# Expert slots divided by token tile, and a spare buffer that holds one expert matrix of each layer

## The chip, the core and the metric

One core of one Trainium2 chip runs the whole program. The time is the device time of one execution in microseconds. The engines are TensorE (PE, its weight loads are shown as PEld), VectorE (DVE), ScalarE (ACT), GpSimd (POOL) and SyncE (SP), which here issues nearly all DMAs. All data is fp32.

## What is computed

The reference is an encoder of two layers over 256 tokens of width 1024. Each layer adds a mixer (layer 0: gated spatial mixing beside windowed attention; layer 1: dilated attention), a cross-attention to 256 memory tokens, and a mixture of experts. The last is what the change touches:

```python
def hier_moe(h, w_grp, b_grp, w_exp, b_exp, w_gate, w_up, w_down):
    t = h.reshape(-1, d)
    grp = jnp.argmax(g_logits, axis=-1)
    top_v, top_i = lax.top_k(e_sel, MOE_TOP_K)
    ...
    for gi in range(MOE_GROUPS):
        hid = jax.nn.silu(jnp.einsum('td,edf->tef', t, w_gate[gi])) * jnp.einsum('td,edf->tef', t, w_up[gi])
        hid = hid * gate[:, gi, :, None]
        y = y + jnp.einsum('tef,efd->td', hid, w_down[gi])
```

Each of the 16 experts of a layer has three matrices (gate and up 1024x512, down 512x1024) of 2.097 MB each, 48 matrices a layer. A token goes to two experts.

## The kernel before

Tokens lie in two tiles of 128 (`h`, `nrm`, dimension t). Weights come through a **ring** of six slots of 16 KB per partition, one matrix each. `load(n, ...)` on SP waits until slot n - 6 has been used (`ring_used`) and issues the DMA; TensorE waits in `arrived` for its landing, and its last product that reads the slot raises `ring_used`. SP's loads stand in one order for the whole program, so a load that waits holds back all behind it. The same slots serve both mixers, the cross-attentions and the experts.

**The expert stage** (`experts(l)` on each engine). The router gives every token two experts; `pos{l}` counts, by products with a triangular and an all-ones matrix (5 matmuls, in two tiles), which place a token has in its expert's list. VectorE's `selectors_of(g)` builds `sel`, for each tile the 0/1 matrix from 128 tokens to the 4 x 64 slots of a group's experts. `gather(g, j)` multiplies token rows by it: 4 matmuls of 256 columns into bank 6 or 7 (a "piece"), both tiles summed. VectorE or ScalarE copies a piece, scaled, into `xg`. Pieces use the two banks in turn, so a piece waits for the copy of the last but one.

Then come eight **duos** q of two experts, two duos to a group g. In a duo TensorE computes gate products into bank 0 and up products into bank 1 (`products`, 16 matmuls each, 64 slots of either expert in half of the bank's partitions), then two pieces of the next group's gathers, four flips (transposes) of `hid` into bank 2, and the down products into banks 3 and 4. ScalarE computes silu and copies the left half of the output (512 columns) to `ysb`, VectorE computes `hid` and copies the right half. Each duo's outputs are added to the tokens by four **scatters** (two tiles, two halves, 128x512 each, line 1362), with `scat`, the transposed and gated selectors of the duo. They run during the next duo, three behind its gate products (`before_up`; in duos 6 and 7 behind the up products, `before_turn`) and one behind its flips; VectorE adds each to `h` (line 1657). The outputs of duo 7 are scattered at the end of the stage (`halves_of_first` and three more), and the next norm waits for them.

Where an expert has more than 64 tokens, a flag (`ovf`) lets a second pass run over all experts with their weights loaded anew. It doesn't run here.

In the trace a matmul of 128x512 or 128x256 is two instructions, one of flips is one. Line 1009 is the helper `mm`, 1012 the helper `flip`, 752 ScalarE's copy.

## Time and profile before

| | |
|---|---|
| time of the runs, us | 1103.21, 1104.18, 1105.98 (median 1104.18) |
| profiled execution: its own time | 1105.44 |
| its span, granted TensorE clock | 1103.6, 0.984 |
| PE busy | 1040.9 (94%) |
| DVE, ACT busy | 269.2 (24%), 170.6 (15%) |
| read from HBM | 280.76 MB, 255 GB/s over the span |
| chain that ended last | PE 90%, DMA 5%, DVE 3% |
| expert stage of layer 0, products | from 243.85 to about 471.8 us |
| expert stage of layer 1, products | from 861.78 to about 1089.7 us |

The page gives one execution: the busy time of each engine, the span cut into 40 slices of 27.6 us, the DMA queues, and the chain of work that ended last. The trace behind it has every instruction with its start, what it waited for, and the clock that TensorE was granted.

### The profile page before, as it was taken

What the parts mean: (1) busy time and instruction counts of PE and PEld (TensorE: products, weight loads), DVE (VectorE), ACT (ScalarE), POOL (GpSimd) and SP (SyncE); (2) the same over time, 40 slices, a digit from 0 to 9 for tenths busy, and PEclk for the clock granted to TensorE, in tenths of its full rate; (3) what the DMA queues carried; (4) which work ended last, traced back from release to release, by engine and by line L of the source; (5) the groups of instructions that cost most, each with busy time, mean ns of one, the idle gap of its engine ahead of it and who ended that gap; (6) DMA issues with size and microseconds to landing.
All of it is one profiled execution on the core that took longest, in us unless ns stands there. A gap on an engine that the chain in (4) does not pass through costs nothing.

```text
span 1103.6 us, 10945 instructions
## 1 busy us (share of the span) xinstructions
PE 1040.9 (94%) x4480; PEld 619.9 (56%) x4480; DVE 269.2 (24%) x688; ACT 170.6 (15%) x354; POOL 11.1 (1%) x21
## 2 busy tenths in 40 slices
PE   4999998999999999899999999999978999999986
PEld 4567566464444443377788877886555544334432
DVE  2424332340111111132212221122335111111114
ACT  2014302031111110011101120101022210111101
POOL 1020000000000000000000000000000000000000
PEclk8999999999999999999999999999998999999998
DMA  9684234228999999998094490874322499999991
GB/s 332 225 292 153 77 153 171 77 77 361 425 428 428 426 427 429 373 249 210 1 254 117 88 280 2 207 265 171 120 110 77 194 429 422 426 429 429 427 426 55
DMA packets 108359, 282.54 MB, mean 256 GB/s; under 512 B 3847, under 2 KB 81751, under 8 KB 96025
## 3 DMA queue, kind: packets, MB, share of 16 engines
q1 hardware_dynamic: 106864, 278.17, 68.0%
q0 software_dynamic: 1168, 3.40, 1.0%
q8 instruction: 34, 0.56, 0.2%
q10 hardware_dynamic: 280, 0.31, 0.1%
q14 instruction: 13, 0.10, 0.0%
HBM read 280.76 MB, written 1.11 MB: 255 GB/s over the span
## 4 chain that ended last, share of the span: by engine, by line
PE 90%; DMA 5%; DVE 3%; issue 1%; ACT 0%; DVEq 0%; SPq 0%
PE banks L1009 83%; PE banks L1362 5%; DMA ring<-expert_w_up_in 3%; PE banks L1012 3%; DMA ring<-xkv_w_in 1%; DVE nrm L1779 0%; DVE mx L1771 0%; DVE h L1649 0%; DVE nrm L1722 0%; DVE nT L665 0%; DVE scratch L1813 0%; ACT nT L663 0%; DVE xv L692 0%; DVE scratch L2020 0%; DVE xkT L699 0%
## 5 line engine op out<-in xcount | busy, mean ns | idle before, releaser
L1009 PE MATMUL banks<-ring,scratch 128*64 128x512 f32 (+1 forms) x1792 | 454.1, 599 | 13.7 <-issue 6.0
L1009 PEld LDWEIGHTS banks<-ring,scratch 128*64 128x64 f32 (+1 forms) x1792 | 169.3, 146 | 283.2 <-issue 281.1
L1009 PE MATMUL banks<-nT,ring 128*128 128x256 f32 x1040 | 227.0, 379 | 1.5 <-DVE nT L665 0.6
L1009 PEld LDWEIGHTS banks<-nT,ring 128*128 128x128 f32 x1040 | 196.6, 190 | 28.7 <-issue 1.9
L1009 PE MATMUL banks<-ring,nT 128*128 128x384 f32 (+2 forms) x320 | 102.7, 476 | 0.0
L752 ACT ACTIVATE scratch<-banks 128x512 f32<-128x512 f32 (+1 forms) x76 | 42.6, 583 | 282.4 <-PE banks L1012 167.8
L1009 PEld LDWEIGHTS banks<-ring,nT 128*128 128x128 f32 x320 | 57.4, 190 | 37.7 <-issue 7.7
L1657 DVE TENSOR_TENSOR h<-banks,h 128x512 f32<-128x512 f32 x56 | 38.7, 691 | 117.3 <-PE banks L1362 117.3
L1009 PE MATMUL banks<-scratch,nrm 128*128 128x256 f32 x256 | 61.1, 394 | 2.4 <-DVE scratch L1948 1.2
L1009 PEld LDWEIGHTS banks<-scratch,nrm 128*128 128x128 f32 x256 | 48.8, 195 | 19.0 <-issue 12.5
L1362 PE MATMUL banks<-scratch 128*128 128x512 f32 x112 | 56.8, 619 | 0.0
L2013 DVE TENSOR_TENSOR scratch<-banks,scratch 128x512 f32<-128x512 f32 x16 | 16.8, 1052 | 152.3 <-PE banks L1009 152.3
L1009 PE MATMUL banks<-scratch 128*128 128x128 f32 (+4 forms) x324 | 49.0, 324 | 4.1 <-issue 2.3
L1009 PEld LDWEIGHTS banks<-scratch 128*128 128x128 f32 (+2 forms) x324 | 40.3, 185 | 17.5 <-issue 8.2
L851 ACT ACTIVATE scratch<-banks,gains 128x256 f32<-128x256 f32 x56 | 23.5, 470 | 158.2 <-PE banks L1009 158.2
L2020 DVE TENSOR_SCALAR scratch<-banks 128x512 f32<-128x512 f32 x16 | 11.1, 692 | 116.1 <-PE banks L1009 116.1
L1009 PE MATMUL banks<-scratch,ring 128*128 128x256 f32 x128 | 31.0, 404 | 5.4 <-DMA ring<-xkv_w_in 5.4
L1012 PE MATMUL banks<-cst,scratch 128*128 128x128 f32 x180 | 26.7, 286 | 8.5 <-DMA scratch<-mem_in 8.5
L1362 PEld LDWEIGHTS banks<-scratch 128*128 128x128 f32 x112 | 17.9, 189 | 28.6 <-issue 18.1
L1012 PEld LDWEIGHTS banks<-cst,scratch 128*128 128x128 f32 x180 | 23.0, 149 | 16.7 <-issue 14.0
L1009 PEld LDWEIGHTS banks<-scratch,ring 128*128 128x128 f32 x128 | 25.9, 204 | 10.3 <-DMA ring<-xkv_w_in 5.8
L1649 DVE TENSOR_TENSOR h<-banks,h 128x512 f32<-128x512 f32 x24 | 16.6, 691 | 53.2 <-PE banks L1009 53.1
(148 smaller groups left out, 421.9 us busy)
## 6 DMA issues: line engine op xcount, KB each, us to landing
ring<-expert_w_gate_in SPq DMA_DIRECT2D x32, 2048.0 KB, 13.1
ring<-expert_w_up_in SPq DMA_DIRECT2D x32, 2048.0 KB, 14.3
ring<-expert_w_down_in SPq DMA_DIRECT2D x32, 2048.0 KB, 11.7
ring<-odd_w_in_in SPq DMA_DIRECT2D x72, 512.0 KB, 7.1
ring<-xkv_w_in SPq DMA_DIRECT2D x4, 2048.0 KB, 11.8
ring<-even_w_in_in SPq DMA_DIRECT2D x3, 2048.0 KB, 20.3
ring<-even_w_out_in SPq DMA_DIRECT2D x2, 2048.0 KB, 16.2
ring<-xq_w_in SPq DMA_DIRECT2D x2, 2048.0 KB, 11.8
```

The lines of the kernel that those rows point to most:

```text
L752: return nc.scalar.activation(dst, src, ACT.Copy)
L851: last = nc.scalar.activation(xg[:, g % 2, c, :], pbank(k)[:, i * 256:(i + 1) * 256], ACT.Copy, scale=gtok[:, l, c:c + 1])
L1009: return giving_back(nc.tensor.matmul(dst, lhsT, rhs, start=start, stop=stop))
L1012: return giving_back(nc.tensor.transpose(dst, src, ident))
L1362: nc.tensor.matmul(pbank(k)[:, :], rows, ysb[:, q % 2, f * 512:(f + 1) * 512], start=True, stop=True).then_inc(piece_ready, 1)
L1649: v.tensor_tensor(r, b[:, :], r, ALU.add).then_inc(resid, 1)
L1657: v.tensor_tensor(r, pbank(k)[:, :], r, ALU.add).then_inc(evac[k % 2], 1)
L2013: v.tensor_tensor(hid.rearrange("p c f -> p f c"), bank[1].rearrange("p (f c) -> p f c", c=FC), silu.rearrange("p (f c) -> p f c", c=FC), ...
L2020: v.tensor_scalar(ysb[:, q % 2, 512:D], bank[4][:, :], 1.0, None, ALU.mult).then_inc(y_dve, 1)
```

## The change

1. **Slots by tile.** The 64 slots of an expert are divided, 32 (`SHARE`) for either token tile. A gather of a tile then fills only its own columns: 4 matmuls of 128 columns in a piece, nothing summed. `sel` has half the size. The flag is raised where an expert has more than 32 tokens in one tile.
2. **Scatter once per group.** As only 32 x 4 = 128 slots of a group belong to a tile, the outputs of both duos of a group lie in one tile of 128 rows in `ysb[:, t]`, and four scatters serve a group. They run in duos 2, 4 and 6 (`closes_group`) and at the end. `scat` has two transposed blocks per group in place of four.
3. **Output copies by tile.** ScalarE copies tile 0's rows, VectorE tile 1's: for either expert of the duo 32 partitions by 1024 columns from banks 3 and 4.
4. **Positions.** Two matmuls of 32 columns in place of five of 16.
5. **Spare slot.** The room that this frees, the last 16 KB of `scratch`, holds matrix 6 of each layer (gate of the third expert, used in duo 1). Its load stands ahead of the stage's ring loads in SP's order, waits in layer 0 for the mixer's last outputs and gated rows, in layer 1 for the use of the spare matrix of layer 0. The ring carries 47 matrices of a layer, in the old order.
6. The second pass takes one tile at a time.

```diff
 SLOTS = 64
+SHARE = SLOTS // TILES
...
+        assert a.at <= SCRATCH - SLOT
+        spare_slot = scratch[:, SCRATCH - SLOT:SCRATCH]
...
+        MATRICES = 3 * EXPERTS
+        SPARE = 6
+        W_ODD = W_MOE0 + MATRICES - 1
...
+        def closes_group(q):
+            return q >= 2 and q % 2 == 0
+
         def before_up(q):
-            return range(3) if 1 <= q < 6 else ()
+            return range(3) if closes_group(q) and q < DUOS - 2 else ()
 
         def before_turn(q):
-            return range(3) if q >= 6 else ()
+            return range(3) if closes_group(q) and q == DUOS - 2 else ()
...
+                if l == 0:
+                    sp.wait_ge(ya_set, 2)
+                    sp.wait_ge(e_pv_ps, PAIRS)
+                else:
+                    sp.wait_ge(gate_ps, 2)
+                sp.dma_start(spare_slot, rows_of(SPARE)).then_inc(spare_in, 16)
+                for m in range(MATRICES):
+                    if m != SPARE:
+                        load(ring_index(l, m), matrix(l, m), rows_of(m))
...
+        def expert_rows(half, i, t):
+
+            to, at = SHARE * (2 * half + i), SLOTS * i + SHARE * t
+            return ysb[to:to + SHARE, t, :], banks[at:at + SHARE, 3:5, :].rearrange("p b n -> p (b n)")
...
-                    copy(ysb[:, q % 2, 0:512], bank[3][:, :]).then_inc(y_act, 1)
+                    for i in range(2):
+                        dst, src = expert_rows(half, i, 0)
+                        last = copy(dst, src)
+                    last.then_inc(y_act, 1)
...
                     for i in range(2):
                         for t in range(TILES):
-                            last = mm(pbank(k)[:, i * 256:(i + 1) * 256], nrm[:, t, 2 * j + i, :],
-                                      sel[:, t, 256 * g:256 * (g + 1)], t == 0, t == 1)
+                            at = i * SEQ + t * P
+                            last = mm(pbank(k)[:, at:at + P], nrm[:, t, 2 * j + i, :], sel[:, t, P * g:P * (g + 1)], True, True)
...
                 selectors_of(0)
-                v.tensor_reduce(most, pbank(k)[:, 32:48], AX.X, ALU.max).then_inc(evac[PIECES[k] % 2], 1)
+                v.tensor_reduce(most, pbank(k)[:, 32:64], AX.X, ALU.max).then_inc(evac[PIECES[k] % 2], 1)
                 selectors_of(1)
                 piece_out(dve, k)
-                step(v.tensor_scalar(most, most, SLOTS + 0.5, None, ALU.is_gt))
+                step(v.tensor_scalar(most, most, SHARE + 0.5, None, ALU.is_gt))
```

How the instructions of layer 0's expert stage stand on TensorE, first before. Rows 1 and 2 of each piece are the positions and the first group's gathers; after them `ring,scratch` are gate, up or down products (16 each), `scratch,nrm` gathers, `cst,scratch` flips, and line 1362 (1402 in the change) scatters. The piece of before goes to the end of duo 2's gathers:

```order
L1009 MATMUL banks<-scratch,cst 128x16 x5
L1009 MATMUL banks<-scratch,nrm 128x256 x16
L1009 MATMUL banks<-ring,scratch 64x512 x32
L1009 MATMUL banks<-scratch,nrm 128x256 x8
L1012 MATMUL banks<-cst,scratch 128x128 x8
L1009 MATMUL banks<-ring,scratch 64x512 x32
L1362 MATMUL banks<-scratch 128x512 x3
L1009 MATMUL banks<-ring,scratch 64x512 x16
```

Behind it stand, in every duo, three scatters, gathers, flips and the fourth scatter. In the change the same place, up to duo 1, and then, behind a break, duos 2 and 3:

```order
L1056 MATMUL banks<-scratch,cst 128x32 x2
L1056 MATMUL banks<-scratch,nrm 128x128 x16
L1056 MATMUL banks<-ring,scratch 64x512 x32
L1056 MATMUL banks<-scratch,nrm 128x128 x8
L1059 MATMUL banks<-cst,scratch 128x128 x6
...
L1402 MATMUL banks<-scratch 128x512 x3
L1056 MATMUL banks<-ring,scratch 64x512 x16
L1056 MATMUL banks<-scratch,nrm 128x128 x8
L1059 MATMUL banks<-cst,scratch 128x128 x4
L1402 MATMUL banks<-scratch 128x512
L1059 MATMUL banks<-cst,scratch 128x128 x2
L1056 MATMUL banks<-ring,scratch 64x512 x48
```

The gathers have half the columns, duo 1 has no scatters, and the last row (down of duo 2, gate and up of duo 3) runs through where three scatters stood between gate and up.

SP's order of DMAs ahead of and into the first expert stage, before:

```order
L479 DMA ring<-xkv_w_in 128x8x512
L479 DMA ring<-expert_w_gate_in 128x4096 x2
L479 DMA ring<-expert_w_up_in 128x4096 x2
L479 DMA ring<-expert_w_down_in 128x4096 x2
L479 DMA ring<-expert_w_gate_in 128x4096 x2
```

and in the change:

```order
L501 DMA ring<-xkv_w_in 128x8x512
L546 DMA scratch<-expert_w_gate_in 128x4096
L501 DMA ring<-expert_w_gate_in 128x4096 x2
L501 DMA ring<-expert_w_up_in 128x4096 x2
L501 DMA ring<-expert_w_down_in 128x4096 x2
L501 DMA ring<-expert_w_gate_in 128x4096
```

The spare load is new ahead of the stage's first loads, and duo 1's gates take one ring load in place of two. In layer 1 the same row stands behind the load of xo_w.

## Rows read from the trace of the kernel before

**Rows 1.** The page: busy tenths of TensorE, and GB/s, in 40 slices.

```profile
PE   4999998999999999899999999999978999999986
GB/s 332 225 292 153 77 153 171 77 77 361 425 428 428 426 427 429 373 249 210 1 254 117 88 280 2 207 265 171 120 110 77 194 429 422 426 429 429 427 426 55
```

**Rows 2.** A stretch: its us, busy us by engine, clock, DMA share, GB/s.

```profile
275.00:300.00 25.00, 24.72 (x108) 10.71 (x106) 4.56 (x7) 3.36 (x7) 0.00 (x0) 1.00 1.01 429
```

**Rows 3.** Timeline of TensorE in layer 0's stage: start us, us, engine, what.

```profile
279.81 7.09 PE L1009 MATMUL banks<-ring,scratch 128*64 128x512 f32 x32
...
367.38 7.09 PE L1009 MATMUL banks<-ring,scratch 128*64 128x512 f32 x32
...
441.91 7.09 PE L1009 MATMUL banks<-ring,scratch 128*64 128x512 f32 x32 [0.43 <-DMA ring<-expert_w_gate_in]
451.69 8.78 PE L1009 MATMUL banks<-ring,scratch 128*64 128x512 f32 x32 [2.69 <-DMA ring<-expert_w_up_in]
460.40 3.04 PE L1362 MATMUL banks<-scratch 128*128 128x512 f32 x6
...
464.71 5.80 PE L1009 MATMUL banks<-ring,scratch 128*64 128x512 f32 x26
```

**Rows 4.** Waits of TensorE, total us, times, longest: layer 0 twice, layer 1 last.

```profile
PE banks L1009 <- DMA ring<-expert_w_up_in: 2.7, 1, 2.7
...
PE banks L1009 <- DMA ring<-expert_w_gate_in: 0.4, 1, 0.4
...
PE banks L1009 <- DMA ring<-expert_w_gate_in: 0.3, 1, 0.3
```

**Rows 5.** The chain that ended last, 240 to 470: start us, us, what.

```profile
432.86 18.69 DMA ring<-expert_w_up_in
```

**Rows 6.** Timeline of SP's DMA issues, whole span.

```profile
150.35 0.82 SPq L479 DMA_DIRECT2D ring<-expert_w_gate_in  x2
...
739.23 0.37 SPq L479 DMA_DIRECT2D ring<-xo_w_in  x1
745.82 13.65 SPq L479 DMA_DIRECT2D ring<-expert_w_gate_in  x2
```

**Rows 7.** Layer 0's mixer: timeline of TensorE, and stretch with GB/s last.

```profile
134.87 1.08 PE L1009 MATMUL banks<-scratch 128*64 128x256 f32 x8
...
125.00:150.00 25.00, 25.00 (x77) 11.35 (x76) 4.30 (x15) 2.90 (x6) 0.00 (x0) 1.00 0.00 1
```

**Rows 8.** Timeline of TensorE at the starts of both expert stages.

```profile
220.93 4.16 PE L1009 MATMUL banks<-rw,nT 128*128 128x20 f32 x32 [0.37 <-ACT nT L663]
...
233.21 1.18 PE L1009 MATMUL banks<-scratch,cst 128*128 128x16 f32 x10
235.59 7.29 PE L1009 MATMUL banks<-scratch,nrm 128*128 128x256 f32 x32 [1.19 <-DVE scratch L1948]
243.85 1.51 PE L1009 MATMUL banks<-ring,scratch 128*64 128x512 f32 x6 [0.97 <-issue]
...
851.69 9.12 PE L1009 MATMUL banks<-scratch,nrm 128*128 128x256 f32 x32 [1.19 <-issue]
```

**Rows 9.** Timeline of VectorE there: a selector, and a piece's copy.

```profile
234.73 0.76 DVE L1948 TENSOR_TENSOR scratch<-cst,scratch 128x256 f32<-128x256 f32 x2
...
238.16 0.88 DVE L1981 TENSOR_SCALAR scratch<-banks,gains 128x256 f32<-128x256 f32 x2
```

**Rows 10.** Timelines at the end of layer 0's stage, VectorE and ScalarE.

```profile
471.85 0.69 DVE L2020 TENSOR_SCALAR scratch<-banks 128x512 f32<-128x512 f32 x1 [6.38 <-PE banks L1009]
...
475.41 1.06 ACT L766 ACTIVATE nrm<-h 128x1024 f32<-128x1024 f32 x1 [2.96 <-DVE h L1649]
```

**Rows 11.** Stretches as in rows 2: the granted clock is the last but two.

```profile
454.00:456.00 2.00, 2.00 (x8) 0.82 (x6) 0.00 (x0) 0.00 (x0) 0.00 (x0) 0.50 1.00 426
...
845.00:850.00 5.00, 2.84 (x17) 2.75 (x16) 3.04 (x27) 3.78 (x4) 0.00 (x0) 0.54 0.25 105
850.00:855.00 5.00, 3.81 (x11) 3.10 (x11) 3.38 (x18) 0.00 (x0) 0.00 (x0) 0.50 0.00 0
```

More of the change, by code:

```diff
@@ L358, in encoder @@
         landed_at, level = [], [0] * RING
-        for i in range(W_MOE1 + GROUPS * PER_GROUP):
+        for i in range(W_MOE1 + MATRICES - 1):
             level[i % RING] += 16 * PARTS.get(i, 1)
@@ L365, in arrived, with ring_index, matrix, matrix_in @@
             eng.wait_ge(landed[n % RING], landed_at[n] + later)
+        def ring_index(l, m):
+            return None if m == SPARE else W_MOE[l] + m - (m > SPARE)
+        def matrix(l, m):
+            return spare_slot if m == SPARE else slot(ring_index(l, m))
+        def matrix_in(eng, l, m):
+            if m == SPARE:
+                eng.wait_ge(spare_in, 16 * (l + 1))
+            else:
+                arrived(eng, ring_index(l, m))
         PIECES = {}
@@ L1323, in experts @@
                 b = pbank(k)
-                m0, m1 = (mask[:, t].rearrange("p g e -> p (g e)") for t in range(TILES))
-                mm(b[:, 0:16], earlier, m0, True, True)
-                mm(b[:, 16:32], ones, m0, True, False)
-                mm(b[:, 16:32], earlier, m1, False, True)
-                mm(b[:, 32:48], ones, m0, True, False)
-                mm(b[:, 32:48], ones, m1, False, True).then_inc(piece_ready, 1)
+                both = mask.rearrange("p t g e -> p (t g e)")
+                mm(b[:, 0:TILES * EXPERTS], earlier, both, True, True)
+                mm(b[:, TILES * EXPERTS:2 * TILES * EXPERTS], ones, both, True, True).then_inc(piece_ready, 1)
                 def gather(g, j):
@@ L1408, in experts @@
                     for i in before_turn(q):
-                        scatter(q - 1, i)
+                        scatter(g - 1, i)
                     pe.wait_ge(hid_sb, x + 1)
@@ L1428, in experts @@
                             for i in range(2):
-                                w = slot(n + 4 + i).rearrange("p (c n) -> p c n", c=FC)
+                                w = matrix(l, m + 4 + i).rearrange("p (c n) -> p c n", c=FC)
                                 last = mm(bank[3 + f][SLOTS * i:SLOTS * (i + 1), :],
@@ L1449, in second_pass @@
                 with pe.If(flag > 0):
-                    for i in (2, 3):
-                        piece_out(pe, f"scatter{l}{DUOS - 2}{i}")
                     pe.wait_ge(s["added"], 1)
@@ L1485, in second_pass @@
                             pe.wait_ge(s["y_sb"], e * 2 + k + 1)
-                            for t in range(TILES):
-                                for f in range(2):
-                                    last = mm(bank[(5, 0, 6, 7)[2 * t + f]][:, :], scatr[:, t * P:(t + 1) * P],
-                                              yrest[:, f * 512:(f + 1) * 512], True, True)
+                            for f in range(2):
+                                last = mm(bank[(5, 0)[f]][:, :], scatr, yrest[:, f * 512:(f + 1) * 512], True, True)
                             last.then_inc(s["proj"], 1)
@@ L2015, in experts @@
                     for i in before_turn(q):
-                        add_rows(l, q - 1, i)
-                    if q:
-                        add_rows(l, q - 1, 3)
+                        add_rows(l, g - 1, i)
+                    if closes_group(q):
+                        add_rows(l, g - 1, 3)
                     dve.wait_ge(y_ps, x + 1)
-                    v.tensor_scalar(ysb[:, q % 2, 512:D], bank[4][:, :], 1.0, None, ALU.mult).then_inc(y_dve, 1)
+                    for i in range(2):
+                        dst, src = expert_rows(half, i, 1)
+                        last = v.tensor_scalar(dst, src, 1.0, None, ALU.mult)
+                    last.then_inc(y_dve, 1)
                 second_pass(l, flag)
```

167 lines of the change are left out of this document (78 added, 89 removed).

## Prediction

> **What bounds the kernel now.** I read the page's 40 slices first: TensorE is busy in nine tenths or more of nearly every slice, but in two stretches, the two expert stages, the row of GB/s stands at 422 to 429 as well [rows 1]. So these stages have two resources at their limit at once. A stretch of 25 us inside the first of them shows TensorE busy for 24.72 us and a DMA share of 1.01 beside it [rows 2]. One expert matrix has 2.097 MB; at 428 GB/s that is 4.90 us, and a duo (two experts, six matrices) needs 29.4 us of DMA. Of TensorE the timeline shows what a duo needs there: the up products of four duos in a row start at 279.81 (the first) to 367.38 (the fourth), 29.2 us apart [rows 3]. TensorE and the DMA stream are thus within 0.2 us per duo of each other, and the stream is the slower. The prefetched ring (six matrices) hides that until the last duo. Only there does TensorE wait for weights, 2.7 us in layer 0 and, in an equal row, in layer 1, and 0.4 and 0.3 us ahead of the gate pair [rows 4], and the chain that ended last goes over to the DMA there: the last up pair landed at 432.86 + 18.69 = 451.55 [rows 5]. Work that is taken off TensorE in an expert stage therefore uncovers a DMA bound at once. What counts is when the stream of ring loads starts, how many matrices it has, and what follows its end.
>
> **The spare matrix.** Its load takes 2.097 MB out of the stream of each layer, 4.9 us. The cost is hidden if it lands in idle DMA time and holds nobody up. In layer 0 it stands in SP's queue right ahead of the first gate loads, which went out at 150.35 when the output projection gave up its slots [rows 6]. It waits for the last pair's outputs, which TensorE has finished at 135.9 [rows 7]. From 125 to 150 the DMA engines moved 1 GB/s [rows 7], so it lands near 144, and the SP queue is free again before 150. In layer 1 it follows the load of xo_w at 739.23, 6.6 us ahead of the gate loads at 745.82 [rows 6]. Behind it only those are queued, and their matrices are used after the gathers, which end at 860.8 [rows 8]. Both cost nothing, and if the cover were gone, a load behind it would be 4.9 us later at most. In each expert stage 41 ring loads are left of the 42 that came after the prefetched six.
>
> **The earlier start.** The ring loads of the stage begin when the first gate products give up their slots: products from 243.85 in layer 0 [rows 8], the loads one pair's products, 7.1 us, later. Before the products come the positions, the selectors and 16 gathers. (1) Positions: five matmuls (ten instructions, 1.18 us [rows 8]) become two (four). Their length is nearly free of the column count: 32 instructions of 20 columns took 4.16 us, 0.13 each [rows 8]. So 0.5 us, 0.65 less. (2) Selectors: two VectorE operations, 0.76 us [rows 9], become one over as many elements, 0.38 less. It comes twice ahead of the first copy out of the banks. (3) Gathers: 32 instructions with 256 columns, 7.29 us, 0.23 each [rows 8], get 128 columns. This form does not occur here with these operands. By columns it would be 0.11, by the 20-column row 0.13, and at worst it stays 0.23. I take 0.13, as the weight load doesn't shrink: 1.04 us for a piece of eight. Four pieces would then be 3.1 us shorter, but the third has to wait for VectorE's copy of the first, which starts at 238.16 [rows 9], now 0.65 + 0.38 + 0.38 earlier, and ends at 237.6. Then two pieces (2.1) and the last copy (0.88 for a piece [rows 9], here ScalarE's) with two short hops give products from 240.9 instead of 243.85: **3.0 us** in layer 0, with bounds of 1.4 (gathers no shorter) and 4.1 (no wait for the copy). In layer 1 the same stretch ran mostly at the lower clock, 0.50 to 0.54 granted from 845 to 855 [rows 11], and the gathers took 9.12 us for 7.29 [rows 8]. With the positions at half the clock, the same steps give 4.3 there; since the clock's level there is uncertain, I take 4.0.
>
> **The duos in between.** TensorE loses four of eight scatters in a group of two duos (six instructions of three scatters take 3.04 us [rows 3], so some 1.0 each), 1.5 us of gathers per duo (16 instructions at 0.23 [rows 8] against 0.13) and two flips of 0.15. A group falls from 58.4 to about 51.1 us of TensorE, while the stream still needs 58.8. So this gain of about 26 us per layer is not paid out. It only makes TensorE wait, from about the fifth duo on, up to 2.8 us ahead of a pair (a pair lands every 9.8 us, and its products take 7.0). VectorE saves 16 additions per layer, ScalarE half a copy: neither is on the path.
>
> **The end of the stream.** Loads start 3.0 earlier and are one fewer, so the last up pair lands at 451.55 - 3.0 - 4.9 = 443.65 and the last down pair 9.8 later, at 453.45. Before, the down products started at 464.71, 3.3 us after their landing: the up products took 8.78 us instead of 7.09, and then came three scatters (3.04), flips and one scatter [rows 3]. Duo 7 has no scatters now. After the up products (7.1) come VectorE's product (1.05), flips (0.6), ScalarE's copy (0.6) and the hops, so TensorE could start at about 453.4, level with the landing: 11.2 us earlier. The long up products are a matter of the clock. It was granted at 0.50 from 454 to 456 [rows 11], right behind the wait of 2.7, and that cost the 1.7 us; behind the wait of 0.4 the products took 7.09, as ever [rows 3]. The new wait of 2.8 is like the former, so I count one such fall in the last duo: **9.5** us in layer 0.
> [...]
>
> **The copies of the expert outputs.** The two copies of 128x512 (VectorE's takes 0.69, ScalarE's beside it less [rows 10]) become two of 32x1024 on each engine. VectorE takes 0.44 for 256 columns (0.88 for two [rows 9]) and 0.69 for 512, so about 1.2 for 1024; ScalarE took 1.06 for 128x1024 [rows 10]. If partitions don't matter, two take 2.35 instead of 0.69. Within the stage they lie beside the next gate products. Behind the last duo the last scatters wait for them: **1.65 us lost** per layer. Bounds: 0.6 (time with the partitions, one overlapping the other) and 4 (the two engines, now in the same banks, one after the other).
>
> **Sum.** Layer 0: 3.0 and 4.9 at the landing, 1.6 net at the down products (11.2 - 1.7 less 7.9), 1.65 back: 7.85. Layer 1 with 4.0 for 3.0: 8.85. Together 16.7 us off the span of 1103.6. The profiled run itself took 1105.44, and the median of the runs, 1104.18, lies 0.6 above its span; the same distance gives **1087.5**. The odd layer and both mixers stay as they are: their loads hang on the same slots as before.
>
> **Rivals.**
> (a) *No falls of the clock in the last duos.* Another 1.7 us in each layer: 1084. For it: the phase of the clock's changes shifts. Against: both layers had the wait of 2.7 us at the same place before [rows 4], and 2.8 is no shorter.
> (b) *Start gains lost.* If the copies out of the banks, not TensorE, pace the gathers, or the new ones are no shorter, of the 7.0 us at the two starts some 1 to 2 remain; or the 32-partition copies cost their upper bound. Time 1091 to 1095. For it: ScalarE and VectorE alternate on two banks, and the third gather waits for a copy even before.
> (c) *TensorE's whole saving is paid out.* Per layer 16 us of scatters, 9 of gathers, 1 of flips and 3 at the start: 1104 - 58 = 1046. The stream would have to move six matrices in 26 us, 484 GB/s, against 429 at a share of 1.01 [rows 2].
> (d) *Slower: the clock stays low in the DMA-bound duos.* The place is the second half of each expert stage. A wait of 2.8 us absorbs a fall that costs 1.7, and the point from which it decides is a fall that costs more than the wait, that is, one that lasts over 5.6 us. At the start of layer 1's stage it did last some 10 us, with TensorE busy 2.84 and 3.81 of 5 us [rows 11]. That would cost 5 us, 2.2 above the wait, at each of 11 pairs a layer: 1087.5 + 48 = 1136. Against it: a pair's products keep TensorE busy for 7 us without a gap, as in the fall at 452, which ended within them.
> (e) *The second pass runs*, since a slot list now overflows from 33 tokens of one tile instead of 65 of both. It would run 32 rounds a layer with three matrices each, 14.7 us of DMA at least: over 900 us more. Counted from the reference's own inputs, the fullest share of a tile is 31 tokens (51 and 52 are the fullest of both tiles), so it stays out, two tokens short of it.
> (f) *Nothing moves*: the stream finds a new wait, for instance on the slot given back singly in duo 1. The stream has always at least two matrices queued there (pairs are issued every 7 to 12 us, and take 9.8), which speaks against it.
>
> **How the numbers follow.** The forecast, 1087.5 (own range 1085 to 1090), has 0.45; (a) 0.25; (b) 0.18; (c) 0.02; (d) 0.04; (e) 0.01; (f) 0.05. The range 1081 to 1095 takes in the forecast, (a) and (b), with the unknown copies and gathers at their ends, and leaves out little more than a tenth. About 0.3% (3.3 us) is what a measurement of this kernel can tell from no change. Faster 0.91, within it 0.04, slower 0.05.
>
> **What would show it.** The load of the spare matrix near 136 and 740, landed before 150 and 750. First products near 240.9. Waits of TensorE for ring loads in the second half of both expert stages, some 20 us a layer in place of 3.1, with the DMA share still 1.00 at 428 GB/s up to about 453. Down products of duo 7 at 453 to 455. Copies of 32x1024 near 1.0 and 1.2 us, and the last scatters about 2.5 us behind the products. Wrong would be: DMA idle inside the stage, a clock below 1.00 for most of its second half, a higher rate than 430 GB/s, or any instruction of the second pass.

## The result, and the profile after

The changed kernel takes **1091.59 us** in the median of 4 runs (1090.81 to 1096.08), the kernel before 1105.08 beside it. The ratio is 0.9885, with a 95% interval of 0.9854 to 0.9915. The profiled execution took 1091.02, with a span of 1089.2 against 1103.6: 14.4 us less, where 16.7 were forecast. The medians are 13.5 us apart. The time lies in the wide range of 1081 to 1095 and outside the forecast's own range of 1085 to 1090.

The rows that answer to [rows 1], [rows 2] and the stretch of [rows 7], of the page and of stretches, read now:

```profile
PE   4999998989998988789999999999978999997884
GB/s 332 232 296 155 78 232 149 91 88 356 428 428 426 428 429 427 365 254 187 1 231 146 55 284 37 169 252 307 38 194 78 182 428 430 424 430 427 427 414 39
...
275.00:300.00 25.00, 23.86 (x112) 10.22 (x110) 5.60 (x7) 4.79 (x8) 0.00 (x0) 1.00 1.01 427
125.00:150.00 25.00, 25.00 (x77) 11.33 (x76) 4.35 (x14) 2.90 (x6) 0.00 (x0) 1.00 0.22 84
```

In the two expert stages the DMA rate is where it was, 424 to 430 GB/s, and TensorE has given up its full digits: the stream alone is at its limit. The 84 GB/s between 125 and 150 are the spare matrix (2.1 MB; its last packet ended at 143.3), where 1 GB/s flowed before [rows 7]. SP's timeline has its issue (columns: start us, us):

```profile
136.11 0.34 SPq L546 DMA_DIRECT2D scratch<-expert_w_gate_in  x1
150.40 0.82 SPq L501 DMA_DIRECT2D ring<-expert_w_gate_in  x2
...
734.46 0.51 SPq L546 DMA_DIRECT2D scratch<-expert_w_gate_in  x1
740.63 13.63 SPq L501 DMA_DIRECT2D ring<-expert_w_gate_in  x2
```

The gate loads behind it go out as before: 150.40 against 150.35 in layer 0, and in layer 1 740.63 against 745.82 [rows 6], the 5.2 us that the kernel is ahead there. TensorE's timeline of layer 0's stage, to be laid beside [rows 3 and 8]:

```profile
233.26 0.53 PE L1056 MATMUL banks<-scratch,cst 128*128 128x32 f32 x4
234.65 2.02 PE L1056 MATMUL banks<-scratch,nrm 128*128 128x128 f32 x16 [0.86 <-DVE scratch L1983]
237.93 2.02 PE L1056 MATMUL banks<-scratch,nrm 128*128 128x128 f32 x16 [1.25 <-DVE scratch L2016]
240.93 13.95 PE L1056 MATMUL banks<-ring,scratch 128*64 128x512 f32 x64 [0.98 <-DVE scratch L2016]
...
384.42 8.78 PE L1056 MATMUL banks<-ring,scratch 128*64 128x512 f32 x32 [2.71 <-DMA ring<-expert_w_up_in]
...
413.78 7.09 PE L1056 MATMUL banks<-ring,scratch 128*64 128x512 f32 x32 [2.70 <-DMA ring<-expert_w_up_in]
...
443.17 8.59 PE L1056 MATMUL banks<-ring,scratch 128*64 128x512 f32 x32 [2.71 <-DMA ring<-expert_w_up_in]
452.91 0.66 PE L1059 MATMUL banks<-cst,scratch 128*128 128x128 f32 x4 [1.15 <-DVE scratch L2046]
454.41 7.09 PE L1056 MATMUL banks<-ring,scratch 128*64 128x512 f32 x32 [0.84 <-issue]
464.15 3.68 PE L1056 MATMUL banks<-scratch 128*128 128x256 f32 x10 [2.65 <-DVE scratch L2055]
470.08 3.60 PE L1059 MATMUL banks<-cst,h 128*128 128x128 f32 x16 [2.25 <-issue]
```

The products of 7.09 us ran at the full clock, those of 8.78 or 8.59 partly at half of it. The last row, the flips (transposes) of layer 1's first norm, has no row ahead of the prediction to answer to. These are the kernel before's, from the same view:

```profile
472.68 3.68 PE L1009 MATMUL banks<-scratch 128*128 128x256 f32 x10 [0.88 <-DVE scratch L2020]
476.20 2.04 PE L1012 MATMUL banks<-cst,h 128*128 128x128 f32 x16
478.72 3.48 PE L1009 MATMUL banks<-nT,ring 128*128 128x256 f32 x15 [0.49 <-DVE nT L661]
```

Before, the flips followed the scatters without a gap and took 2.04 us. Now TensorE stands still for 2.25 us that no engine and no DMA ends ("issue"), and the flips take 3.60. The start of layer 1's stage and the end:

```profile
851.15 13.96 PE L1056 MATMUL banks<-ring,scratch 128*64 128x512 f32 x64 [0.97 <-DVE scratch L2016]
...
1053.38 8.78 PE L1056 MATMUL banks<-ring,scratch 128*64 128x512 f32 x32 [2.70 <-DMA ring<-expert_w_up_in]
1064.89 7.09 PE L1056 MATMUL banks<-ring,scratch 128*64 128x512 f32 x32 [0.93 <-issue]
1074.62 5.20 PE L1056 MATMUL banks<-scratch 128*128 128x256 f32 x10 [2.65 <-DVE scratch L2055]
```

Counted along TensorE, the distance to the kernel before grows and shrinks like this (its other times: down products of layer 1 at 1082.58, last scatters at 1090.55, router products at 842.11 against 835.67 now):

| place | ahead by, us | this step |
|---|---|---|
| first products, layer 0 | 2.9 | +2.9 |
| last down products, layer 0 | 10.3 | +7.4 |
| last scatters start | 8.5 | -1.8 |
| behind the flips of layer 1 | 5.2 | -3.3 |
| router of layer 1 | 6.4 | +1.2 |
| first products, layer 1 | 10.6 | +4.2 |
| last down products, layer 1 | 17.7 | +7.1 |
| last scatters start | 15.9 | -1.8 |
| end | 14.4 | -1.5 |

Waits of TensorE in layer 0's stage (total us, times, longest), where [rows 4] had 2.7 and 0.4:

```profile
PE banks L1056 <- DMA ring<-expert_w_up_in: 9.4, 4, 2.7
PE banks L1056 <- DMA ring<-expert_w_gate_in: 4.7, 3, 1.9
...
PE banks L1056 <- DMA ring<-expert_w_down_in: 1.1, 1, 1.1
```

### The profile page after: what moved, and what is told of

Same layout as the page of the kernel before. It is cut to its first block, busy times and chain, and to the rows that moved or that the text cites. A ratio compares the mean times of both kernels' runs of the same rounds, so it can differ in the third digit from the quotient of the medians.

```text
span 1089.2 us, 10736 instructions
## 1 busy us (share of the span) xinstructions
PE 988.5 (91%) x4388; PEld 596.7 (55%) x4388; DVE 270.2 (25%) x656; ACT 192.0 (18%) x370; POOL 11.1 (1%) x21
## 4 chain that ended last, share of the span: by engine, by line
PE 74%; DMA 19%; DVE 3%; issue 2%; ACT 0%; DVEq 0%; SPq 0%
PE banks L1056 70%; DMA ring<-expert_w_up_in 14%; DMA ring<-expert_w_gate_in 3%; PE banks L1059 3%; PE banks L1402 2%; DMA ring<-xkv_w_in 1%; DVE nrm L1812 0%; DVE mx L1804 0%; DVE h L1682 0%; DVE scratch L2055 0%; DVE scratch L2046 0%; DVE nrm L1755 0%; DVE scratch L2016 0%; DVE nT L697 0%; DVE scratch L1846 0%
## 5 line engine op out<-in xcount | busy, mean ns | idle before, releaser
L1056 PEld LDWEIGHTS banks<-ring,scratch 128*64 128x64 f32 (+1 forms) x1760 | 174.9, 147 | 298.8 <-issue 294.4
L796 ACT ACTIVATE scratch<-banks 128x512 f32<-128x512 f32 (+2 forms) x92 | 63.8, 713 | 285.6 <-PE banks L1059 168.5
L2055 DVE TENSOR_SCALAR scratch<-banks 32x1024 f32<-32x1024 f32 x32 | 39.1, 1223 | 134.3 <-PE banks L1056 134.1
L1056 PE MATMUL banks<-scratch 128*128 128x128 f32 (+5 forms) x356 | 64.5, 353 | 7.6 <-DVE scratch L2055 5.3
L1056 PEld LDWEIGHTS banks<-scratch 128*128 128x128 f32 (+2 forms) x356 | 45.6, 184 | 29.8 <-issue 16.7
L1056 PEld LDWEIGHTS banks<-scratch,nrm 128*128 128x128 f32 x256 | 32.1, 204 | 13.1 <-issue 13.1
L1056 PE MATMUL banks<-scratch,nrm 128*128 128x128 f32 x256 | 34.9, 294 | 3.0 <-DVE scratch L2016 1.3
L1682 DVE TENSOR_TENSOR h<-banks,h 128x512 f32<-128x512 f32 x24 | 16.6, 691 | 54.7 <-PE banks L1056 54.6
L786 ACT ACTIVATE scratch<-banks,roots 128x384 f32<-128x384 f32 x16 | 9.3, 581 | 99.6 <-PE banks L1056 99.6
L1690 DVE TENSOR_TENSOR h<-banks,h 128x512 f32<-128x512 f32 x24 | 16.6, 691 | 37.2 <-PE banks L1402 37.2
L910 ACT ACTIVATE scratch<-banks 128x512 f32<-128x512 f32 x16 | 9.6, 597 | 90.7 <-PE banks L1056 90.7
```

What stands on the lines that cost most here:

```text
L786: last = nc.scalar.activation(ov[:, par, kind - 3, :], b[:, 0:CG * P], ACT.Copy, scale=class_roots[:, kind - 3:kind - 2])
L796: return nc.scalar.activation(dst, src, ACT.Copy)
L910: nc.scalar.activation(silu, bank[0][:, :], ACT.Silu).then_inc(silu_sb, 1)
L1056: return giving_back(nc.tensor.matmul(dst, lhsT, rhs, start=start, stop=stop))
L1682: v.tensor_tensor(r, b[:, :], r, ALU.add).then_inc(resid, 1)
L1690: v.tensor_tensor(r, pbank(k)[:, :], r, ALU.add).then_inc(evac[k % 2], 1)
```

## Experiments

### Is the end of the stage set by the number of ring loads?

`no_spare`: the changed kernel, all 48 matrices of a layer through the ring again.

```diff
-        SPARE = 6
-        W_ODD = W_MOE0 + MATRICES - 1
+        SPARE = -1
+        W_ODD = W_MOE0 + MATRICES
```

> The changed kernel without the spare matrix: all 48 matrices of a layer go through the ring, the slots by tile, the scatters per group and the copies by tile stay. Theory A (the stream of ring loads bounds both expert stages, a matrix is 4.9 us of it): each stage ends 4.9 us later than in the change, so 1091.6 + 9.8 = 1101, TensorE waits for ring loads some 5 us longer in each layer, and the gain over the kernel before is only about 4 us. Theory B (TensorE's shorter work is what pays): the spare matrix is worth nothing, 1091 to 1093.

Measured: 1100.75 (1098.92 to 1105.18, 10 runs), ratio 0.9966 (0.9935 to 0.9998). The matrix is worth 9.2 us by the medians (8.9 by the two ratios), 4.6 a layer, against one load of 4.90. Everything else in the change, by itself, brings about 4 (0.2 to 7.2 by the interval). In layer 0 that kernel waits 10.4, 8.8 and 2.3 us for up, gate and down weights, 21.5 against 3.1 in the kernel before: most of TensorE's saving of 26 us stands in its trace as waits and is not paid.

`spare_only`: the kernel before, its slots and scatters as they were, with the spare matrix alone (the room comes from the second pass's buffers).

```diff
-        xrest = a.take(CH * P).rearrange("p (c s) -> p c s", c=CH)
-        yrest = a.take(D)
+        xrest = ysb[:, 0].rearrange("p (c s) -> p c s", c=CH)
+        yrest = ysb[:, 1]
...
+        SPARE = 6
```

> The kernel before with the spare matrix alone; the room comes from buffers of the second pass, which share room with others of the stage. Slots, gathers, scatters and copies are those of before. Theory A: TensorE needs 29.2 us for a duo and the stream, one matrix shorter, no longer holds it up in the last duo. The waits of 0.4 and 2.7 us and the fall of the clock behind them (1.7) go: 4.8 us a layer, 1095.5 in all. Theory B (TensorE's shorter work pays, the stream is hidden anyway): no change, 1104 to 1106.

Measured: 1105.15 (1100.39 to 1108.55, 10 runs), ratio 0.9999 (0.9973 to 1.0024). One load fewer per layer is worth nothing here in the median (theory B), with an interval of 2.7 us to either side. The stretches of that kernel show why (last two columns: DMA share, GB/s):

```profile
270.00:280.00 10.00, 10.00 (x48) 3.81 (x45) 0.69 (x1) 0.66 (x2) 0.00 (x0) 1.00 1.01 429
280.00:290.00 10.00, 10.00 (x39) 3.20 (x40) 2.12 (x4) 0.54 (x1) 0.00 (x0) 1.00 1.00 401
290.00:300.00 10.00, 9.72 (x46) 5.64 (x47) 1.71 (x2) 2.17 (x5) 0.00 (x0) 1.00 0.98 385
300.00:310.00 10.00, 10.00 (x47) 3.84 (x43) 1.36 (x3) 1.20 (x2) 0.00 (x0) 1.00 0.83 319
```

TensorE is full and the DMA engines run short: 429, then 401, 385 and 319 GB/s. Against 428 that is 1.8 MB, or 4.2 us of the stream, out of the 4.9 that the missing load saves. A ring of six slots is refilled as TensorE gives them back. With one matrix less to load, the stream catches up with TensorE in the second and third duo and waits for slots, and the time it lost there it needs at the end, where TensorE still waits 1.9 us for the last up pair. What the load is worth within the stage is small too: from the first products to the last down products this trace takes 217.8 us in layer 0, that of `before_no_second` below, which like this one has no fall of the clock in the stage, 219.1. So a TensorE that gives slots back faster makes the missing load worth its 4.9 us, and the missing load makes a faster TensorE worth its time. The forecast priced them one after the other. By the ratios they are worth 4 and 0 us alone, and 13 together; the 9 us between are clear of the noise, about 5.6 us for the three ratios together.

`busy_duos`: the changed kernel with 12 matmuls of 128x512 on constants per layer, four in each of duos 1, 3 and 5, that is part of the work that the change took off TensorE.

```diff
+                    if q in (1, 3, 5):
+                        idle_products(4)
```

> The changed kernel with twelve more matmuls of 128x512 on constants per layer, four behind the gate products of duos 1, 3 and 5, into a bank that nobody reads: 0.86 us each, 10.3 us of TensorE work per layer, less than the 26 us that the change took out. Theory A (the stream bounds the stages, TensorE's work lies in its waits): no change, 1090 to 1093, and TensorE's waits for ring loads are 8 to 10 us shorter per layer. Theory B (TensorE's work is on the path): 20.6 us more, 1112.

The 24 matmuls of both layers are some 20.6 us of TensorE (32 records, 16 matmuls, of this form take 14.0, or 0.87 each). Measured: 1098.43 (1093.1 to 1105.24, 10 runs), ratio 0.993 (0.9902 to 0.9957): 6.8 us more than the changed kernel by the medians, 5.0 by the ratios, so between the two theories. In layer 0 the last down products start at 459.19 in its trace instead of 454.41; 0.9 of that is a later start of the stage, 3.9 arose in it (3.5 in layer 1). The stream ran short early in the stage here too:

```profile
280.00:300.00 20.00, 18.87 (x98) 8.47 (x96) 3.93 (x4) 4.19 (x7) 0.00 (x0) 1.00 0.99 393
290.00:310.00 20.00, 20.00 (x88) 7.33 (x86) 4.95 (x6) 2.62 (x3) 0.00 (x0) 1.00 0.99 409
```

In the changed kernel the rate is 427 or more over these stretches. So "TensorE's saving is not paid out" holds for its bulk, but a quarter to a third of the added work was paid. The place where the stream loses is in the first duos: while the ring still has its lead, TensorE's work there decides when the next slot comes back. The shortfall from 280 to 300, 35 GB/s or 0.7 MB, is only 1.6 us of the stream, though; where the rest of the 3.9 us comes from, this run does not show.

### The gap behind the last scatters

`before_no_second` and `after_no_second`: either kernel without the second pass, which stands in the program as a branch on a flag that is never raised by these inputs, over 78 matmuls on TensorE.

```diff
-                second_pass(l, flag)
+                pass
```

> The kernel before without the code of the second pass, which never runs on these inputs, and without the branch over it. Control for the next kernel. Both theories: within 1 us of the kernel before, since its flips of the next norm start right behind the last scatters (at 476.20).

> The changed kernel without the code of the second pass and the branch over it. In the changed kernel TensorE stood still for 2.25 us at 467.8 in front of the flips of layer 1's first norm, with no wait that the profile shows, and these then ran at the lower clock (3.60 us in place of 2.04). Theory C (TensorE waits for its instructions behind the branch): the gap and the fall go, 3.5 us less, 1088. Theory D (the gap hangs on data, on additions or on the squares of the norm): the gap stays, 1091 to 1092.

Measured: 1106.01 (1100.94 to 1110.15, 10 runs), ratio 1.0008 (0.9981 to 1.0036) without it in the kernel before, and 1093.17 (1092.34 to 1094.16, 4 runs), ratio 0.9889 (0.9834 to 0.9944), in the changed one. The latter's timeline:

```profile
465.53 5.34 PE L1056 MATMUL banks<-scratch 128*128 128x256 f32 x10 [2.65 <-DVE scratch L2055]
470.71 2.04 PE L1059 MATMUL banks<-cst,h 128*128 128x128 f32 x16
```

The gap is gone, so it belongs to the branch. The fall of the clock did not go with it: the scatters take 5.34 us in place of 3.68 and the flips 2.04 in place of 3.60, so it only came one group earlier. From the start of these scatters to the first products of layer 1 (473.54 and, here, 473.23) this trace takes 7.70 us in place of 9.39, 1.7 less. The medians don't show it: theory C's 1088 did not come, and 1093.17 lies 1.6 above the changed kernel. Its stage starts 1.3 us later and it has one more fall of the clock in layer 1's cross-attention (806.8 us). I come back to the gap below.

### Does a wait filled with work save the clock's fall?

`fill_last`: three matmuls on constants ahead of the last up products, in the wait of 2.7 us.

```diff
+                    if q == DUOS - 1:
+                        idle_products(3)
```

> The changed kernel with three matmuls of 128x512 on constants behind the gate products of duo 7, 2.6 us, in the place of the wait of 2.7 us there. Theory E (the clock falls because of that wait, and only this fall costs time, as the down products then start 1.4 us behind their landing): the last up products take 7.1 instead of 8.6 to 8.8 us in both layers and the down products start at their landing; 1.3 us less per layer, 1089. Theory F (the falls come from elsewhere or don't matter): 1091 to 1093, products as long as before.

Measured: 1092.95 (1090.23 to 1098.41, 4 runs), ratio 0.9887 (0.9833 to 0.994). Timeline of layer 0:

```profile
441.11 2.84 PE L1056 MATMUL banks<-cst 128*128 128x512 f32 x6
443.88 7.09 PE L1056 MATMUL banks<-ring,scratch 128*64 128x512 f32 x32
...
453.69 8.78 PE L1056 MATMUL banks<-ring,scratch 128*64 128x512 f32 x32 [0.90 <-DMA ring<-expert_w_down_in]
465.13 3.68 PE L1056 MATMUL banks<-scratch 128*128 128x256 f32 x10 [2.65 <-DVE scratch L2061]
471.27 3.54 PE L1059 MATMUL banks<-cst,h 128*128 128x128 f32 x16 [2.47 <-issue]
```

The up products take 7.09 as at the full clock, and the down products 8.78: in this trace, in layer 1 as in layer 0, a fall came one wait later instead. Theory E's 1089 did not come. That the filling moved the fall is likely but not shown, because falls come and go between these kernels with nothing filled. The kernel before without its branch has the same wait and no fall in either stage:

```profile
452.41 7.09 PE L1009 MATMUL banks<-ring,scratch 128*64 128x512 f32 x32 [2.71 <-DMA ring<-expert_w_up_in]
```

### The terms at both ends of the stage

`gates_later`: VectorE's ten small gate steps (1.7 us) behind its copies of the gathers instead of ahead of them. In the changed kernel the second half of the gathers waits 1.25 us for the first of these copies, which starts at 236.91.

```diff
-                dve.wait_ge(r_in, 2 * l + 2)
-                dve.wait_ge(r_exp, 2 * l + 2)
...
                 for j in (0, 2):
                     k = PIECES[f"gather{l}0{j}"]
...
+                dve.wait_ge(r_in, 2 * l + 2)
+                dve.wait_ge(r_exp, 2 * l + 2)
```

> The changed kernel with VectorE's ten small steps for the gates moved behind its two copies of gathers, so that the copy of the first piece starts when the piece is there (235.8 instead of 236.91 in layer 0). Theory A (whatever starts the stream earlier is paid out in full at the end of the stage): gate products 1.1 us earlier, last landing 1.1 us earlier, 2.2 us less over both layers, 1089.4. Theory B (the stream has slack at its start): the first products come earlier, the last landing doesn't, 1091 to 1092.

Measured: 1091.42 (1089.85 to 1095.17, 4 runs), ratio 0.9863 (0.982 to 0.9906): no gain in the median. In the trace the wait is 0.17 instead of 1.25:

```profile
238.55 2.02 PE L1056 MATMUL banks<-scratch,nrm 128*128 128x128 f32 x16 [0.86 <-DVE scratch L1983]
240.74 2.02 PE L1056 MATMUL banks<-scratch,nrm 128*128 128x128 f32 x16 [0.17 <-DVE scratch L2000]
243.74 6.66 PE L1056 MATMUL banks<-ring,scratch 128*64 128x512 f32 x30 [0.97 <-DVE scratch L2000]
```

From the gathers' start to the products it is 5.19 us in place of 6.28. So the third gather did wait for VectorE, as forecast; 1.1 us in one layer is below what the runs tell apart, and whether it is paid out (theory A or B) stays open. In layer 1, where the gathers run at the lower clock and take 6.2 us in one piece, they never waited for the copies, and nothing was to be had.

`early_copies`: the copies of the last outputs in two halves of 512 columns, the first beside the second half of the down products, and the last scatters waiting for each tile by itself.

```diff
-                    act.wait_ge(y_ps, x + 1)
...
+                    for f in range(2):
+                        act.wait_ge((left_ps, y_ps)[f], x + 1)
+                        for i in range(2):
+                            last = copy(*expert_rows(half, i, 0, f))
...
-                pe.wait_ge(y_act, x)
-                pe.wait_ge(y_dve, x)
+                pe.wait_ge(left_act, x)
```

> The changed kernel with the output copies in halves: the left 512 columns of both experts are copied (32x512, two on each engine) while TensorE computes the right 512, and each of the last scatters waits only for its own tile's copies. Theory G (the copies of 32x1024 behind the last down products cost 2.65 us in each layer): the first of the last scatters starts at once, the last one about 2.3 us earlier, 4.6 us less over both layers, 1087. Theory H (the next norm waits for something else): the scatters come earlier, the total stays at 1091 to 1092.

Measured: **1087.08** (1083.91 to 1093.69, 4 runs), ratio 0.9848 (0.9796 to 0.99). Timeline of layer 0:

```profile
454.82 7.09 PE L1058 MATMUL banks<-ring,scratch 128*64 128x512 f32 x32 [0.84 <-issue]
461.84 1.13 PE L1058 MATMUL banks<-scratch 128*128 128x256 f32 x4
463.19 2.84 PE L1058 MATMUL banks<-scratch 128*128 128x512 f32 x6 [0.22 <-ACT scratch L798]
469.51 2.82 PE L1061 MATMUL banks<-cst,h 128*128 128x128 f32 x16 [3.47 <-issue]
```

The wait of 2.65 is gone, the scatters follow at once, and part of it, 1.2 us, goes into a longer gap ahead of the flips. The median is 4.5 us below the changed kernel's, as theory G had it. The ratios (0.9848 and 0.9885) are 4.1 us apart with overlapping intervals, so the trace shows the wait gone and the runs leave its worth rough. The trace has luck in it too: in layer 1 its last up products take 7.09 us, without the fall of the clock that made them 8.78 in the changed kernel.

### Both, and the gap again

`early_gates` has both edits.

> The changed kernel with both edits: VectorE's gate steps stand behind its copies of the gathers, and the output copies run in halves of 512 columns beside the last down products. Alone, the second edit took the median from 1091.6 to 1087.1 us, and the first shortened the stretch from the gathers' start to the first products from 6.28 to 5.19 us in each of two layers. If the two add, the median is 1087.1 - 2.2 = 1084.9 (bounds 1083 to 1087.5). If the ring's transfers, which start no earlier for it, take the first one's gain back at the end of the stage, it stays at 1087. The gap ahead of layer 1's first flips should stand at 2.2 to 4.4 us.

Measured: 1085.98 (1082.8 to 1094.53, 6 runs), ratio 0.9864 (0.9825 to 0.9903). Its first products come at 240.96, 5.19 us behind the gathers' start, its gap is 2.13. In layer 1 the first edit does nothing, as said: the expectation of a gain in each layer was wrong. Against `early_copies` alone the 1.1 us are within the spread.

Then the place of the code. TensorE's instructions come in over queue 8 in loads of 16384 bytes. The branch over the second pass has a row of its own in the trace, if one asks for its line. Here it is for the kernel before, the changed one and `early_gates_shift110` (one branch per layer, two in all: shortest, median and longest in ns, then the first and the last start in us; the one ahead of layer 1's flips starts first and took 483, 5714 and 491 ns):

```profile
L1449 PEldq COMPARE_BRANCH  x2: 483/1989/3495, 472.7 to 1090.6; - x2
L1489 PEldq COMPARE_BRANCH  x2: 343/3028/5714, 464.2 to 1074.7; - x2
L1495 PEldq COMPARE_BRANCH  x2: 348/420/491, 470.7 to 1076.8; - x2
```

So this branch took 0.48 us before and 5.71 in the changed kernel. TensorE's queue still works on the last scatters meanwhile, and the gap is what is left of the branch behind them. The list has that branch for all kernels that contain it, with the number of TensorE's matmul records before each event (an ordinary matmul is two records, and the queue is not in the page's timelines), and the gap ahead of the flips:

```
                     load before it us   branch us       its us   next load us   gap us
before               467.7 (1828)        472.7 (1847)    0.48     476.0          none
spare_only           467.3 (1828)        472.6 (1847)    0.46     476.0          none
early_gates_shift110 466.7 (1790)        470.7 (1805)    0.49     474.1          none
after                436.6 (1716)        464.2 (1801)    5.71     467.3          2.25
no_spare             441.9 (1715)        471.1 (1801)    7.47     475.9          4.01
busy_duos            433.6 (1710)        469.0 (1825)    7.11     473.5          2.21
fill_last            437.4 (1716)        465.2 (1807)    5.93     468.2          2.47
gates_later          439.7 (1716)        468.9 (1801)    7.89     474.3          4.43
early_copies         437.6 (1718)        463.4 (1805)    5.93     466.6          3.47
early_gates          437.6 (1718)        461.8 (1805)    4.59     463.7          2.13
early_gates_shifted  436.7 (1686)        470.9 (1805)    6.48     474.7          4.03
```

`early_gates_shifted` and `early_gates_shift110` add waits on a semaphore that has long been set, behind TensorE's first wait for a load.

```diff
-            pe.wait_ge(id_in, 16)
+            for _ in range(1 + 64):
+                pe.wait_ge(id_in, 16)
```

> The same kernel with 64 more waits in TensorE's program, all on a semaphore that has long been set, behind its first wait for a load, where it then idles for 5.56 us anyway. The computation is unchanged; every later TensorE instruction stands 64 places further on. Theory H: the gap ahead of layer 1's first flips (3.47 us in the kernel with the output copies in halves, 2.25 in the changed kernel) is the load of TensorE's next block of instructions, asked for only as the last scatters run, right ahead of the branch over the second pass (queue 8, 16384 bytes, at 466.6 and 467.3; in the kernel before at 467.7, but 5 us ahead of its scatters). The shift puts the block's edge some 32 matmuls earlier, into the down products, so the load at about 463 or earlier is done before the branch, and the gap goes: the flips start within 0.5 us of the last scatter, 2 to 3.5 us earlier, and the median is 1081.5 to 1083.5 if nothing else moves. Rival I: the gap comes from the branch itself, its flag or a wait for the second tile, and not from where the code stands: the gap stays at 2.2 to 4.4 us and the median at the unshifted kernel's.

Measured: 1088.71 (1087.92 to 1095.05, 6 runs), ratio 0.9874 (0.9841 to 0.9906), gap 4.03. Theory H failed as I had put it: the load comes during the branch, 1.2 us behind the last scatter, and not ahead of it. The list says what did move: the load before the branch, 32 records earlier (1718 to 1686), which is too little to bring another load in ahead of it.

> Again the kernel with both edits, and now 110 such waits ahead in TensorE's program instead of 64 (the computation is unchanged). Counted in TensorE's matmuls, queue 8's loads of 16384 bytes come every 110 to 145 (seldom 90), so a block holds some 125. Without a shift the last load ahead of the branch came 91 matmuls before the one at the branch, with 64 waits 124 before it: the edge moved by 33 matmuls as it should, but to right where the branch stands, and the gap stayed at 4.03 us. In the kernel before, which has no gap, a load comes 28 matmuls ahead of the one at the first flips: its branch stands shortly behind an edge. The branch skips 78 matmuls. Theory H2: the gap is absent when the branch and its target lie in one block, that is when the branch comes 0 to some 45 matmuls behind an edge. 110 waits move it there (91 + 55 - 125 = 21 behind): the gap goes, the flips start within 0.5 us of the last scatter, some 2 to 3.5 us earlier, and the median is 1082 to 1084 beside 1085.98 (1082.8 to 1094.5) of the unshifted kernel, if no clock fall moves into the stretch. Rival I: the gap belongs to the branch wherever it stands, and something else spared the kernel before: the gap stays at 2 to 4.4 us and the median at 1085 to 1089.

Measured: **1084.27** (1083.08 to 1090.65, 6 runs), ratio 0.9805 (0.9766 to 0.9844). TensorE's timeline of `early_gates_shifted`:

```profile
470.69 2.84 PE L1058 MATMUL banks<-scratch 128*128 128x512 f32 x6 [0.24 <-ACT scratch L798]
477.56 3.54 PE L1061 MATMUL banks<-cst,h 128*128 128x128 f32 x16 [4.03 <-issue]
```

and that of `early_gates_shift110`:

```profile
470.50 2.84 PE L1058 MATMUL banks<-scratch 128*128 128x512 f32 x6 [0.24 <-ACT scratch L798]
473.18 2.04 PE L1061 MATMUL banks<-cst,h 128*128 128x128 f32 x16
```

With the same work up to the scatters the flips start 4.2 us earlier and take 2.04 instead of 3.54. Between the two medians lie 4.4 us. Against the unshifted kernel it is 1.7, within the spread of either, so the worth of the gap there isn't settled by the medians. The mechanism is: in eleven kernels the branch takes 0.46 to 0.49 us just where it stands 15 to 19 records behind a load, so that the block it skips into is there already. In the eight where it stands 85 to 119 records behind one, it takes 4.6 to 7.9 us, a load starts within it, and the flips start 2.6 to 3.1 us behind that load's start (467.3 to 470.08, 466.6 to 469.51, 463.7 to 466.55, 474.7 to 477.56). The load itself starts 1.9 to 5.4 us after the branch; what decides this part, and with it whether the gap is 2 or 4 us, stays open. The shift touched neither the flag nor any wait near the branch, so these are ruled out.

The Trainium skill (Runtime: NRT & Kernel Launch, section Instruction fetch mechanics) says that a taken branch whose target is outside the blocks held forces a load of it before execution goes on. The runs agree, with 2.6 to 3.1 us from the load's start to the next instruction.

## Why the prediction held, step by step

**The spare matrix** went out at 136.11 and 734.46, landed hidden and held up nobody, as forecast. It had landed at 143.3 (near 144 forecast). Its worth of 4.9 a layer was right in this kernel (4.6 by `no_spare`), but the working treated it as a term that stands by itself; `spare_only` shows that it does not.

**The earlier start** was forecast at 3.0 and 4.0, the products at 240.9. It was 2.9 and 4.2, at 240.93. The 128-column gathers took 2.02 for 16 instructions, 0.13 each, the floor read from the 20-column row. The positions took 0.53 (0.5 forecast).

**The duos in between.** The forecast of "some 20 us a layer" of waits was too high: 15.2 in layer 0. Its claim that nothing of the 26 us is paid out was too strong: in `busy_duos` 5 to 7 of the 20.6 us of added matmuls were paid, in part through the slots that the first duos give back later. And without any of it the spare matrix is worth nothing, as `spare_only` shows, so part of what the forecast booked as the matrix's 9.8 us belongs to both.

**The end of the stream.** Forecast: down products level with their landing and one fall of the clock, 9.5 us earlier, of which 3.0 came from the start, so 6.5. Measured: 7.4 and 7.1. The fall stands in the row of 8.59 and that of 8.78, and before the fall cost the same. The forecast of one fall in the last duo was right in kind for both layers, and rival (a), none, did not come about in this trace. That was luck in part: `before_no_second` has waits of 2.7 and 2.5 us there and products of 7.09 in both layers, and in layer 0 of the changed kernel two of three waits of 2.7 us were followed by a fall. Rival (a)'s 1.7 us a layer lies within what one trace can differ from the next.

**The copies.** Two on VectorE took 2.46, on ScalarE 2.04 (2.35 forecast), at the same time and out of the same two banks, so neither the lower bound (0.6) nor the upper (4) was near, and fewer partitions did not shorten the copy: ScalarE's 32x1024 took 1.02, its 128x1024 took 1.06 [rows 10]. The loss was 1.8 us a layer against 1.65.

**What was missing.** Two terms, both on the other side. (1) The gap of 2.25 us ahead of layer 1's flips, left by a branch that took 5.71 us in place of 0.48, and the fall behind it (3.60 for 2.04): together 3.3 net of a wait of 0.49 that stood behind the flips before: the sentence "the odd layer and both mixers stay as they are" failed at its first instruction. (2) A fall in the very last scatters, 5.20 for 3.68, where I had counted one fall a layer: 1.5 us. Against them stands 1.2 us from a fall that the kernel before had in layer 1's cross attention, and 1.3 us more than forecast from the starts, stages and copies. So 16.7 became 14.4, and 1091.6 came out past the forecast's own range of 1085 to 1090, where rival (b) had put its time, for another reason: the start gains were all there. The terms that came out as forecast are the start, the copies and, in this kernel, the end of the stream. Of the terms it missed, 4.8 us stand against it and 2.5 for it; that they cancel by half is chance.

**The outcome.** Rivals (c), (d), (e) and (f) left no trace. DMA rates stayed at 424 to 430 GB/s, the mean clock from 240 to 470 was 0.99, and no second pass ran.

## What to carry to other kernels

Where two resources finish a stage within one per cent of each other, price a cut of either one only together with the other, and ask what the buffers between them hold: here cuts worth 4 us and 0 us alone were worth 13 together, each within some 3 us. Count what follows the end of the stage as well (the copies ahead of the last consumer, a branch over a cold block of code), because each microsecond taken from the bulk makes these few the path: the lowest median came from starting the copies a half earlier (4 to 5 us, within overlapping intervals) and from moving a branch to just behind a load of its code. And where idle stretches follow each other, don't count on a gain from filling one of them: a fall of the clock may come at the next.

## What the runs showed of the hardware

- A branch over 78 matmuls took TensorE 4.6 to 7.9 us or 0.5, by the place of the code alone, and left a gap of 2.1 to 4.4 us or none. 110 more instructions at the program's start, hidden in a wait for a load, took the gap away. The same can happen at the end of the program, where nothing follows: layer 1's branch took 3.50 us in the kernel before.
- The stream held 424 to 430 GB/s at a DMA share of 1.00 to 1.01 on one core for over 150 us, beside a TensorE that was busy for 95% of a stretch (275 to 300) or 77% (370 to 390).
- Of the eight waits for weights in layer 0's stage (1.0 to 2.7 us), two were followed by the lower clock: those of 2.7 us ahead of the products of 8.78 at 384.42 and of 8.59 at 443.17. The third of 2.7, ahead of the 7.09 at 413.78, was not. Another fall stands behind the gap (3.60 for 2.04). What picks the wait that is followed by one stays open.
- The profile's timeline can place a gap ("issue", with no releaser) but not name it. The row of the branch's own line does: it ends at 469.90 in the changed kernel, 0.2 us ahead of the flips.
